# A decoder step with 32 streamed experts: the last output projection in one half, expert 1's rows selected by TensorE, half of chunk 10 loaded ahead, the list of weights moved

## The reference

```python
x = x + merged @ w['w_out']
hn = rms_norm(x, w['norm_ffn_g'])
# two-level routing: softmax over 4 groups, best group; its 8 experts, best two; weights comb
# every row goes to two of 32 experts:
(jax.nn.silu(xb @ w_gate[e]) * (xb @ w_up[e])) @ w_down[e]
x = x + sum over the row's two experts of comb * y
```

## Time and profile before

| | before |
|---|---|
| median of 3 runs | 976.23 us (976.17 to 977.42) |
| the profiled execution: its time, its span | 977.72 us, 975.9 us |
| PE busy, DVE busy, ACT busy | 938.2 us (96%), 400.7 us (41%), 242.5 us (25%) |
| mean granted TensorE clock | 0.990 |
| HBM read, written | 246.18 MB, 14.58 MB |

### The profile page before, as it was taken

One profiled execution on the slowest core, in us unless ns is written; L12 is line 12 of the kernel. 1 busy time (PEld: TensorE's weight loads), 2 busy tenths in 40 slices (PEclk: granted clock), 3 DMA queues, 4 the chain that ended last, 5 costly groups with the idle time before them and its releaser, 6 DMA issues.

```text
span 975.9 us, 12367 instructions
## 1 busy us (share of the span) xinstructions
PE 938.2 (96%) x4816; PEld 512.8 (53%) x4816; DVE 400.7 (41%) x915; ACT 242.5 (25%) x603; POOL 70.5 (7%) x79
## 2 busy tenths in 40 slices
PE   5999999999999999999989999999999999999996
PEld 4644777777678888855563333333333333333332
DVE  4679778677543345553661241211211112111111
ACT  3432554364532200032221111111111111111111
POOL 0100000000000000002101111001101010110101
PEclk9999999999999999999989999999999999999999
DMA  8620412112112225469359999999999999999995
GB/s 325 222 87 4 169 44 90 49 45 86 44 45 86 87 87 221 146 240 407 140 213 370 388 390 413 422 416 422 418 417 424 418 417 422 417 424 419 425 417 191
DMA packets 34072, 255.29 MB, mean 262 GB/s; under 512 B 8306, under 2 KB 11634, under 8 KB 18888
## 3 DMA queue, kind: packets, MB, share of 16 engines
q1 hardware_dynamic: 29056, 242.45, 61.7%
q0 software_dynamic: 4960, 12.06, 4.5%
HBM read 246.18 MB, written 14.58 MB: 267 GB/s over the span
## 4 chain that ended last, share of the span: by engine, by line
PE 72%; DMA 20%; DVE 4%; ACT 1%; issue 1%; SPq 1%; POOL 0%; POOLq 0%; DVEq 0%; ACTq 0%
PE ps L2040 25%; DMA arena<-in_w_gu 19%; PE ps L2396 14%; PE ps L2423 7%; PE ps L1978 6%; PE ps L2201 5%; PE ps L2298 3%; DMA arena<-in_x 1%; PE ps L2125 1%; PE ps L2099 1%; PE ps L2056 1%; PE ps L2082 1%; PE ps L2406 1%; PE ps L2235 1%; PE ps L2366 1%
## 5 line engine op out<-in xcount | busy, mean ns | idle before, releaser
L2040 PE MATMUL ps<-arena 128*128 128x272 f32 x1120 | 266.7, 394 | 2.6 <-DVE arena L1423 1.0
L2396 PE MATMUL ps<-arena 128*64 128x512 f32 x512 | 231.8, 602 | 9.8 <-DMA arena<-in_w_gu 9.5
L2040 PEld LDWEIGHTS ps<-arena 128*128 128x128 f32 x1120 | 208.9, 190 | 52.3 <-issue 7.0
L2397 PE MATMUL ps<-arena 128*64 128x512 f32 x512 | 231.8, 602 | 0.0
L843 ACT ACTIVATE arena<-ps 128x272 f32<-128x272 f32 (+5 forms) x181 | 86.1, 482 | 364.5 <-PE ps L2040 168.3
L2396 PEld LDWEIGHTS ps<-arena 128*64 128x64 f32 x512 | 66.9, 138 | 146.4 <-issue 120.9
L1780 DVE SCALAR_TENSOR_TENSOR arena<-arena,list_w,ps 64x512 f32<-64x512 f32 x32 | 24.0, 749 | 217.1 <-ACT arena L1118 217.0
L1978 PE MATMUL ps<-arena 128*128 128x512 f32 (+1 forms) x192 | 75.5, 552 | 6.6 <-DVE arena L1215 6.6
L2298 PE MATMUL ps<-arena 128*64 128x512 bf16 (+2 forms) x552 | 73.4, 414 | 0.0
L1118 ACT ACTIVATE arena<-ps,list_w 64x512 f32<-64x512 f32 x32 | 21.8, 682 | 201.1 <-PE ps L2397 201.1
L802 POOL DMA_INDIRECT out_y<-arena,list_i x32 | 45.3, 1414 | 361.7 <-DVE arena L1787 341.7
(11 more groups left out here) (272 smaller groups left out, 785.0 us busy)
## 6 DMA issues: line engine op xcount, KB each, us to landing
arena<-in_w_gu SPq DMA_DIRECT2D x61, 2048.0 KB, 43.6
arena<-in_w_ed SPq DMA_DIRECT2D x30, 2048.0 KB, 46.5
arena<-in_w_pair SPq DMA_DIRECT2D x20, 1024.0 KB, 4.9
arena<-in_w_q SPq DMA_DIRECT2D x2, 2048.0 KB, 15.4
arena<-in_w_out SPq DMA_DIRECT2D x2, 2048.0 KB, 12.6
arena<-in_w_ed SPq DMA_DIRECT2D x8, 512.0 KB, 14.7
arena<-in_w_gu SPq DMA_DIRECT2D x8, 512.0 KB, 22.0
arena<-in_x SPq DMA_DIRECT2D x4, 512.0 KB, 10.7
```

The source lines that it names most:

```text
L2040: ins = mm(out, w[:, k, :], tokens[:, k, :], start=k == 0 and q in "127", stop=k == 3, skip_group_check=q not in "127")
L2396: mm(ps[0:C, 2 + s, :], xT[s][:, j, :], w[:, jj, 1, :], start=j == 0, stop=j == JX - 1)
L2397: ins = mm(ps[64:64 + C, 2 + s, :], xT[s][:, j, :], w[:, jj, 0, :], start=j == 0, stop=j == JX - 1)
```

## The change

It has four parts.

1. The right half of the last tile is projected as one half of 512 columns (`LAST` = 8, no `END`). Its transpose goes to banks 4 and 2 and is copied half by VectorE, half by ScalarE. VectorE's order around the last two tiles is new: `marks` and `hits` are one function again, and the four operations at the end of `choice` that nothing urgent needs are a function of their own, `after_choice`, called later.
2. Expert 1 leaves `GATHERED`: its rows are selected by TensorE into bank 3, in single calls `select_first(1, j)` that stand between the routing steps, and copied by ScalarE (`stage_x(1, 0, 3)`). Expert 0's last tile is selected like the others, and `turn_first` is gone. `first_hots` makes the places of both experts.
3. Chunk 0's first half and chunk 10's second half are loaded into place 0 at the outset; chunk 0's second half goes to two areas of its own (`apart`), on SP's queue ahead of chunk 9, which is loaded whole. Chunk 10's first half follows when half of chunk 0 is used, chunk 11 in two halves. Because `apart[3]` lies over `x_rows`, POOL's first gather also waits for `ga_used`.
4. On TensorE `tile_list(4)` moves behind `gate_up(0)`, and `list_rows` (the weights) behind `gate_up(1)`.

```diff
-GATHERED = tuple(range(1, 9))
+GATHERED = tuple(range(2, 9))
...
+        apart = {2: area(50304, 2, DE), 3: area(52992, 2, DE)}
...
         def chunk_landed(n):
-            return 16 * (n // N_CHUNK + 1) + (16 if n % N_CHUNK == N_CHUNK - 1 else 0) + (16 * (PIECES - 1) if n >= N_CHUNK and in_pieces(n % N_CHUNK + N_CHUNK) else 0)
+
+            extra = 3 if n % N_CHUNK == 0 else 1 if n % N_CHUNK == 1 and n > N_CHUNK else 0
+            return 16 * (n // N_CHUNK + 1 + extra)
...
+        def pieces(n, first, last):
+
+            rows = area(CHUNK_AT[n % N_CHUNK], PIECES, 4096 // PIECES)[:, first:last]
             part, e = chunk_of[n]
             if part < 2:
+                return rows, a["w_gu"][expert_at(e), part][:, first:last].rearrange("p q u n -> p q (u n)")
+            return rows, a["w_ed"][expert_at(e)][:, first:last]
...
-            load_chunk(0)
+            rows, source = pieces(0, 0, 2)
+            sp.dma_start(rows, source).then_inc(chunk_in[0], 16)
+            rows, source = pieces(N_CHUNK, 2, PIECES)
+            sp.dma_start(rows, source).then_inc(chunk_in[0], 16)
...
             sp.wait_ge(out_ready, LAST)
             load_chunk(EARLY + 1)
-            part, e = chunk_of[N_CHUNK - 1]
-            for q in range(2):
-                sp.wait_ge(out_ready, LAST + q + 1)
-                sp.dma_start(w_up(N_CHUNK - 1)[:, 2 * q:2 * q + 2], a["w_gu"][expert_at(e), part][:, 2 * q:2 * q + 2])\
-                    .then_inc(chunk_in[N_CHUNK - 1], 16)
-            sp.wait_ge(x2_ready, END + 1)
...
+            sp.wait_ge(half_moved[2], 80)
+            sp.wait_ge(turned, LAST)
+            sp.wait_ge(ssq2_ready, LAST)
+            sp.wait_ge(parts_taken, len(SPLIT_HALVES))
+            sp.wait_ge(lower_ready, len(SPLIT_HALVES))
+            sp.dma_start(apart[2], a["w_gu"][expert_at(0), 0][:, 2]).then_inc(chunk_in[0], 16)
+            sp.wait_ge(out_ready, LAST + 1)
+            sp.dma_start(apart[3], a["w_gu"][expert_at(0), 0][:, 3]).then_inc(chunk_in[0], 16)
+            load_chunk(N_CHUNK - 1)
+            sp.wait_ge(x2_ready, LAST + 1)
...
             pool.wait_ge(rows_listed, 1)
-            for e in range(-3, NE):
+            pool.wait_ge(ga_used, 1)
+            for e in range(-2, NE):
...
+                if h == LAST:
+                    act.wait_ge(turned, LAST + 1)
+                    copy(x2T[1][:, 2:4], split(ps[:, 2, 0:256], (2, P))).then_inc(x2T_taken, 1)
+                    root2(NT - 1)
...
             act.activation(e_exp, e_diff, ACT.Exp).then_inc(gexp_ready, 1)
+            stage_x(1, 0, 3)
             do_silu(0, 0, root_of(0))
...
-            for j in range(1, NT - 1):
-                add_out(half_no(j, 1))
+            for j in range(1, NT):
+                add_out(j, 1)
...
-                split_half(half_no(j, 1))
+                if j < NT - 1:
+                    split_half(half_no(j, 1))
+                if j == NT - 1:
+                    after_choice(j - 1)
+                    dve.wait_ge(turned, last_half(j) + 1)
+                    dve.tensor_copy(x2T[1][:, 0:2], split(ps[:, 4, 0:256], (2, P))).then_inc(x2T_last, 1)
+                    hits(j - 1)
                 inverse2(j)
-                if j > 1:
-                    marks(j - 1)
+                if 1 < j < NT - 1:
                     hits(j - 1)
-                if j == NT - 2:
-                    add_out(LAST)
                 choice(j)
-            last_mean()
-            add_out(END)
-            marks(NT - 2)
...
+            link(tt(chosen, pick[:, 0, ORDER[NT - 1], 1, 0:1], pick[:, 1, ORDER[NT - 1], 1, 0:1], ALU.add))
+            link(ts(chosen, chosen, float(BIAS), None, ALU.mult))
             hits(NT - 1)
...
+            def select_first(s, j):
+
+                pe.wait_ge(hot_ready, j + 1 if j < NT - 1 else NT + s)
+                return select(s, (j,), 3 * s)
...
             pe.wait_ge(parts_taken, len(SPLIT_HALVES))
             pe.wait_ge(lower_ready, len(SPLIT_HALVES))
+            pe.wait_ge(ssq2_ready, LAST)
+            select_first(1, 0)
+            turn(LAST)
+            tile_ranks(NT - 2)
+            select_first(1, 1)
+            route(LAST)
             pe.wait_ge(ssq2_ready, LAST + 1)
...
+            for j in range(NT - 2):
+                select_first(0, j)
+            tile_list(NT - 2)
+            select_first(0, NT - 2)
+            select_first(1, 2)
             tile_ranks(NT - 1)
-            tile_list(NT - 2)
-            pe.wait_ge(ssq2_ready, END + 1)
-            turn_first()
+            select_first(0, NT - 1).then_inc(picked, 1)
+            select_first(1, NT - 2)
...
+            turn_rows(0)
+            select_first(1, NT - 1).then_inc(picked, 1)
+            gate_up(0, 0, up_no(0, 0), (0, 0))
             tile_list(NT - 1)
-            gate_up(0, 0, up_no(0, 0), (0, 0))
             pe.wait_ge(rows_listed, 1)
             turn_rows(1)
+            gate_up(1, 1, up_no(1, 0), (0, 0))
             pe.wait_ge(hit_ready, NT + 1)
             list_rows(ps[0:C, 4, 0:2 * NE], 1, 2)
-            gate_up(1, 1, up_no(1, 0), (0, 0))
             turn_hid(0, 0)
```

More of the change, by code:

```diff
@@ L218, in build @@
         d_probs = area(23936, 4, 256)
-        w_left, w_quarter = area(0, KD, 512), area(4096, 2, KD, 256)
+        w_out = [area(4096 * c, KD, 512) for c in range(2)]
         last_merged = area(52992, KD, P)
@@ L1096, in _ @@
             take_parts(0)
-            for h in range(1, END + 1):
+            for h in range(1, LAST + 1):
                 square(h)
-                if h >= NT and h != LAST:
-                    root2(h - NT + 1 if h < LAST else NT - 1)
-                if h < END:
+                if h >= NT and h < LAST:
+                    root2(h - NT + 1)
+                if h < LAST:
                     take_turned(h)
@@ L1687, in hot_places, with hits @@
             def hot_places(e, turn, s):
-                above(dve, picked, turn - 1)
+                dve.wait_ge(picked, turn - 1)
                 one_hots(s, mark[:, :, e:e + 1] if isinstance(e, int) else mark[:, :, bass.ds(e, 1)])
-            def marks(j):
+            def hits(j):
                 t = ORDER[j]
@@ L1710, in hits @@
                     first_hots(j)
+                else:
+                    tt(hot_last[:, 1:2, :], across(cc("place"), 1), over(mark[:, j, 1:2], C), ALU.is_equal).then_inc(hot_ready, 1)
+                    after_choice(j)
                 link(dve.tensor_reduce(rank[0:r, :, t], wide[0:r], AX_X, ALU.add))
@@ L1720, in _ @@
             link(dve.memset(e_diff, 0.0))
-            add_out(0)
+            add_out(0, 0)
             half_mean(0)
@@ L1726, in _ @@
             for j in range(1, NT):
-                add_out(half_no(j, 0))
+                add_out(j, 0)
                 if j < NT - 1:
@@ L2212, in turn @@
                 else:
-                    for k in range(width(h) // P):
-                        ins = transpose(ps[:, 4, k * P:(k + 1) * P], x_half(h)[:, k * P:(k + 1) * P], ident)
+                    for k in range(4):
+                        bank, at = (4, k) if h < LAST or k < 2 else (2, k - 2)
+                        ins = transpose(ps[:, bank, at * P:(at + 1) * P], x_half(h)[:, k * P:(k + 1) * P], ident)
                 ins.then_inc(turned, 1)
@@ L2230, in route @@
                 at = 36 * t if c == 1 else 36 * (NT + t)
-                ks = range(KD) if h == 0 else range(4 * c, 4 * c + 4) if h < LAST else range(2 * h - 12, 2 * h - 10)
-                first, last = (ks[0], ks[-1]) if h < LAST else (4, KD - 1)
+                ks = range(KD) if h == 0 else range(4 * c, 4 * c + 4)
                 for k in ks:
-                    rows = dec_x2T[:, k, :] if h == 0 else x2T[(h - 1) % 2][:, (k - ks[0]) % 4, :]
-                    ins = mm(ps[0:ROWS[t], 6, at:at + 36], rows, w_route[:, k, :], start=k == first, stop=k == last)
+                    rows = dec_x2T[:, k, :] if h == 0 else x2T[(h - 1) % 2][:, k % 4, :]
+                    ins = mm(ps[0:ROWS[t], 6, at:at + 36], rows, w_route[:, k, :], start=k == ks[0],
+                             stop=k == ks[-1])
                 ins.then_inc(logit_ready, 1)
@@ L2263, in _ @@
             dec_out()
-            for h in range(1, LAST):
+            for h in range(1, 2 * NT - 1):
                 half_out(h, (0, 1, 2) if h == 1 else (0,))
```

183 lines of the change are left out of this document (61 added, 122 removed).

## The result

The changed kernel took 981.75 us (median of 4 runs, 981.24 to 982.1) beside 976.83 us for the kernel before (4 runs, 976.17 to 978.32): a ratio of 1.0048, 95% interval 1.003 to 1.0065, some 4.9 us slower. A later repeat with more runs gave 978.68 us (10 runs) beside 976.2 us (33 runs), a ratio of 1.0032, 1.0015 to 1.0048. The sign is as forecast (2.1 us slower); the first median lies 0.25 us above the range, the second inside it. The profiled execution took 982.1 us with a span of 980.3 us, 4.4 us longer than before's. Four executions on record took 1.6 to 5.5 ms; they are out of all ratios, and move the medians given here by less than 0.1 us.

A forecast was written before the change was run, and what follows sets the result against it. The chunk stream was taken as the bound, last held up until expert 0's down projection ends: 533.4 at full clock + 2.4 + 0.8 + 2.2 = 538.8. Chunk 14 then lands 2.1 us later: 978.3 us, range 972.5 to 981.5.

The forecast's parts named there:

- The lag of 7.4 us: From the end of expert 0's down projection to chunk 14's landing, if the queue is empty: 7.4 us for 2 MB.
- the early half: Half of chunk 10, 1 MB, loaded early: taken as 0 because the queue runs empty, 2.5 us were it not empty.
- my signs of being wrong: A full clock from 490 to 535 us, or chunk 14 landing 9 us or more after its issue.
- The sum at full clock: First gate/up to the end of expert 0's down projection: 505.5 + 6.9 + 3.6 + 6.9 + 6.1 + 4.4 = 533.4.
- gap 2: TensorE between expert 1's gate/up and expert 0's down projection: 6.1 us where the kernel before had 1.0.
- stretch 1: TensorE at 491.7 to 496 us, little work: clock expected to fall about 496, 2.4 us taken, bounds 0 to 5.2.
- Terms 2 and 3: Half clock from the 3.6 us gap between the gate/ups, 0.8 us; from the 6.1 us gap after them, 1.9 plus 0.3.
- rival 2: Only the 6.1 us gap lowers the clock: down projection ends 535.6, chunk 14 1.1 us faster, 975.1 us; chance 0.15.
- the end move by: The kernel's end was taken to move by as much as chunk 14's landing, 544.1 before, 546.2 forecast: 2.1 us later.
- the 3.0 us: First gate/up matmul forecast at 505.5 at full clock, 3.0 us before the 508.53 of the kernel before.
- about 0.2%: The difference a measurement of this kernel was said to be able to tell, 1.95 us.
- gap 1: TensorE between the gate/ups of experts 0 and 1: 3.6 us forecast, where the kernel before had 2.36.

The follow-up runs named there:

- the lists back: Changed kernel with the lists of rows and weights moved back ahead of the first and second gate/up: 973.76 us; without chunk 10's early half 973.97 us.
- the wait filled: Idle matmuls in TensorE's wait: 7 before the last down projection, changed kernel, 977.47 us (lists inside gate/ups, 971.33); 6 before the last choice, kernel before, 974.11.
- the weights' list back: Changed kernel with only the list of weights moved back ahead of the second gate/up: 975.53 us, ratio to the kernel before 0.9983.

## Why the prediction was right and wrong

**What bounds the kernel: right, with one limit more.** The end of the first down projection did decide when chunk 14 lands in the changed kernel, over an empty queue. The lag of 7.4 us was too short: 8.1 to 9.5 us in the six profiles where the queue was empty. So one of my signs of being wrong, a chunk 14 that lands 9 us or more after its issue, came up in the repeat (9.5 us) over an empty queue and was a bad sign. The 6.8 us estimated from the Trainium skill, "DMA: Bandwidth & Descriptors", section "Anatomy of one DMA", is farther off than my 7.4; the page's fit is for transfers that GpSimd issues, and these are SP's. And a second limit, which I had missed, takes over when the end comes early: in the eight other profiles chunk 14 lands 19.7 to 22.1 us after the issue of chunk 12. It fits that 8.0 us at the down projection are worth 4.2 at chunk 14, and that the early half was worth nothing with the lists back; over the empty queue of the changed kernel no run was made without it.

**The sum at full clock: right from the first gate/up on, in part by cancelling.** From the first gate/up to the end of the first down projection I had 27.9 us, plus 2.2 for the clock in gap 2 alone: 30.1. Measured 30.0, 29.9 and 29.8 in three profiles. The wait for `hidden` was forecast at some 3 us, measured 3.31; the gap between the gate/ups at 3.6, measured 3.2; these 0.4 us make up for the half clock in gap 2, which cost 0.5 more than its 2.2. Two of my sums don't come out of their own terms. From 502.3 the terms 0.6, 0.7, 0.65 and 0.8 lead to 505.05, not to 505.5; measured was 506.2: the last one-hot places came 0.5 us later than forecast, and from their end it took 3.4 us instead of 2.75. And 1.79, 3.17 and 0.93 are 5.9, where I wrote 6.1 for gap 2; measured 6.2, some 0.2 of it by the half clock.

**Clock, stretch 1: the step that failed in the sum.** "(1) 491.7 to 496: two selections, four transposes, 2.4 us of standing" rested on a projection half that ends at 491.7. The prediction shows no working for 491.7. The 10 matmuls that were left, 0.45 us each, lasted to 494.67, the standing was 0.27 us, no clock fell, and the term of 2.4 us was 0. Terms 2 and 3: 0.8 was 0 (1.7, the upper bound, in one other profile), 2.2 was about 2.7 (1.7 and 0.3 in the down projection, 0.6 in the small groups beside it). So the end came at 536.2 instead of 538.8, which was rival 2's stretch ("only the emptiest gap lowers it"). With the longer lag and a first gate/up at 506.2 instead of 505.5 chunk 14 was 0.6 us late instead of 2.1 us, or of that rival's 1.1 us early.

**From chunk 14 to the end: the step that failed in the time.** I let "the end move by" what chunk 14 moves. It moved by 3.8 us more: 1.0 us of it between chunk 14 and the last whole chunk, and 1.1 and 1.5 us by the clock after 927 us, a place that I hadn't priced. The 1.5 us are shown to belong to the execution, not to the change: the same last down projection takes 3.65 or 5.1 to 5.4 us in kernels of both kinds, and it took 3.65 in both profiles with the wait filled. The 1.1 us didn't come back in the repeat, nor did the 1.0 us: from chunk 14 to the last whole chunk it took 411.0 us there, 411.1 in the kernel before and 412.1 in the first profile, and all profiles lie between 409.5 and 412.5 us. What makes this scatter stays open, and so does why the first measurement lies 3 us above the repeat.

**The reference: one execution taken for the kernel.** The half clock of the earlier trace rows before the first expert was no fixed property of the kernel before; it was there in two profiles of three of kernels with that wait. Counted from the issue of chunk 1, the first gate/up starts after 84.7 and 84.8 us in these two, after 82.9 in the third and with the wait filled, and after 82.5 to 82.6 in all ten profiles with the change's selections, none of which shows a fall there. So of the 3.0 us that I forecast at the first gate/up, some 1.9 are the price of that fall and 0.3 the change's own. The mean granted clock of the runs agrees: 0.991 or less in 54 of 100 runs of the kernel before, in none of the 52 of the five kernels with the change's selections and the list of weights ahead of or within the second gate/up. Six idle matmuls in the kernel before gain 0.18% (0.9982) where the change without its moved lists gains 0.30% (0.997), with overlapping intervals: the clock is most of the gain, as far as these runs tell. For the same reason "about 0.2%" was too fine for four runs: the kernel before ranged from 971.4 to 978.5 us in 33 runs on one chip.

**By the sign:** the moved lists cost 0.6% (0.997 to 1.0032), everything else gains 0.3%. The net is a loss as forecast, by gap 2 as I had it, against a gain that I had put at the first gate/up's 3.0 us and that lies in the clock. That the sign came out is in part luck: the 3.0 us that the kernel before has only in some executions and the 2.4 us of stretch 1 that never came nearly cancel in my sum.

## What to carry to other kernels

Before moving a small step off one engine's path, list what is queued behind its consumer: here a list of 1.7 us took with it a copy, a table load, silu and `hidden`, and TensorE stood 3.3 us and then ran slow. Where TensorE has to wait between bursts, try other matmuls in the wait, useful ones or not, but no more than fit: 6 or 7 helped here, and 22 held up the work behind them. And take the reference from several profiles, and compare them from a point ahead of the change: a clock that fell in one may not have fallen in the next.

## What the runs showed of the hardware

The clock fell after the wait of 3.31 us in all five profiles that had it. After shorter waits it was a matter of the execution: after 1.66 and 0.47 us ahead of the last down projection in 8 of 12, after 1.37 us ahead of the last choice in 2 of 3, after 1.8 us in gap 1 in 1 of 4 (and after 1.2 us there with the weights' list back), after 2.0 us for weights near 925 in 1 of 5. The Trainium skill, "TensorE: Matmul & The Clock Gate", section "Why this matters for your kernels", warns of idle gaps between bursts; the long wait agrees with it, and the shorter ones lowered the clock in some executions and not in others. A matmul of 512 bf16 columns into 64 rows of PSUM took 0.22 us (22 in 4.94), as much as a float32 one of the same shape (16 in 3.65), when no second one ran beside it.
